# Hybrid decoder step: the gates and the levels of gated attention between the slots of the mixing projection, and a ring of cached pages that grows from 16 to 20, 24 and 28

## The chip, the cores and the metric

The kernel runs on one core of one Trainium2 chip. The metric is the device time of one execution in microseconds (us). The core has five engines that run side by side, each with its own queue of instructions that it takes in order, and they wait for one another by counting semaphores: TensorE (PE, matrix products and transposes), VectorE (DVE), ScalarE (ACT), GpSimd (POOL) and SyncE (SP, which here only issues transfers). The trace tells PE's weight loads (PEld) apart from its products. TensorE's clock has two levels, 1.2 and 2.4 GHz, and the profile gives the granted clock as a share of the higher one.

## What is computed

One inference step of one layer, for a prompt of 256 tokens and eight samples of 8 new tokens each (320 columns in all), with a model width of 1024:

```
x <- LN(alpha*x + 1/2*(1+g1)*SwiGLU_1(x*(1+s1)+b1))
x <- LN(alpha*x + (1+g2)*W_o[MoBA heads | GLA heads](x*(1+s2)+b2))
x <- LN(alpha*x + 1/2*(1+g3)*SwiGLU_2(x*(1+s3)+b3))
```

The middle sub-layer is the one that matters here. A projection w_mix_in (1024 x 3088) gives, for each token, queries, keys and values of 8 MoBA heads, queries, keys (4 heads of 64) and values (4 of 128) of gated linear attention (GLA), a GLA output gate, and 16 columns from which the forget gates come:

```
qm, km, vm, qg, kg, vg, gg, rg = split(h @ w_mix_in)
qm, km = rope_partial(qm, pos), rope_partial(km, pos)
log_a = log_sigmoid(rg @ w_gk_up + b_gk) / 16
```

MoBA, for a sample: mean of the keys of each block of 256 of the 2048 cached tokens, the three best blocks for each query and head, softmax over these and the new tokens. The cache is paged: 16 pages of 128 tokens for each sample, found through a page table, for K and for V. GLA: within a chunk, weights q_i k_j exp(b_i - b_j) for j <= i, where b is the running sum of log_a, plus a state that each sample brings and takes along. The results are y of prompt and samples, the new K and V rows and the GLA states, all float32.

## The kernel before

All products of weights are made in three parts (high x high, high x low, low x high) with weights and inputs split in a high part, rounded by ACT, and a low part, the remainder, which DVE subtracts. Weights come in "slots" of 1 MB, of which four fit in `raw`. The order of slots is the table at line 73 (A1, F1, O1, A2, MI, MO, F2, O2): conditioning, first feed-forward, its output, more conditioning, then MI, the mixing projection (12 slots, two output tiles of 128 rows each), MO, the output projection of the mixer (4 slots), and the second feed-forward. `high(t)` (ACT) and `low(t)` (DVE, line 1485) split slot t; there are two buffers each of `wh` and `wl`, so that slot n+2 is split when slot n is used. `pair_slot` multiplies a slot on PE: for each of two tiles 16 products with the high part of the weights and 8 with the low one. It puts the tiles in two of the banks B0 to B3; ACT copies them from there to `M`.

During MI, ACT does two copies to `M` and one `high` in each slot, DVE one `low` and, in the first eight slots, two instructions of `stream`, which rebuild the residual X. After the 12 slots stand, in the order of the program:

- the gates: 24 products for the 16 columns ("rg", lines 1026 to 1028), two groups for "z" (line 1034), on ACT an Exp and a Ln, on DVE a minimum, a subtraction and two running sums, which give `bb`
- rope of the eight q and k tiles (line 1040 on PE, 1952 to 1954 on DVE), and "nat": nine groups of transposes that turn V of GLA, V and K of MoBA back to token rows (lines 1047, 1054)
- the attention of the samples, in four pairs i of samples, into which all the rest is woven in 20 numbered steps, `mix(0)` to `mix(19)`

For one pair PE does, for j = 0 to 3: `turn_keys` twice (4 pages each, one for each sample of the pair, 16 transposes, line 823, copied to `kT` by ACT or DVE as `on_act` says), then `scores(i, j)` (line 834). DVE reduces the scores (`block_values`), then `choose(i)` picks the blocks, ACT makes the exponentials (`exps`), PE turns the probabilities (`turn_probs`, line 854) and multiplies them with the V pages (`values(i, 0)`, `values(i, 1)`, 16 pages each, line 872), and `pick_heads` with `out_high` and `out_low` writes the result to Hh and Hl. The order interleaves pairs: `values(i, 0)`, keys (i+1, 2), `values(i, 1)`, scores (i+1, 2), keys (i+1, 3), scores (i+1, 3), keys (i+2, 0) and so on.

The steps of `mix(k)`: 0 to 6 are causal attention of the prompt (scores, softmax, turned probabilities, values). 7 to 12 are the six "levels" of GLA: at level lv PE multiplies scaled keys with scaled queries (`level`, line 927, two groups "ga" of banks), DVE applies a mask and adds (`level_masks`, lines 1835 and 1847), multiplies the next level's factors (`level_qk`, 1819, 1822) and forms the one after (`level_diff`, 1807, 1812, 1813), and ACT takes two exponentials (`level_exps`). 13 to 19 are GLA's output and state.

Two tables set what waits for what. `FILLS` is the list of all fills of the five banks B3 to B7 that this stage shares in turn: a fill waits until the bank's fill five before was read. `PAGE_GROUPS` is the order in which SP loads the pages, 64 groups of 4 pages (1 MB, four transfers of 256 KB). The pages land in `ring`, 16 pages or 4 groups; group n waits until group n-4 was used, and SP takes the groups strictly in order (`load_pages`, line 548). The ring lies where `raw` lay, so the first groups wait for the last slots of MI. `M`, 24 x 320 elements a partition, and `W`, 9088 elements, hold the mixer's data.

The line that holds the ring's rule:

```
                    if kind == "k":
                        sp.wait_ge(tp_filled, FILL_AT[("k", i, g, bi, 3)] + 1)
                    else:
                        sp.wait_ge(v_used, v_index(i, bi, g) + 1)
```

## Time and profile before

| | us |
|---|---|
| median of 3 runs | 1030.9 (1025.99 to 1033.26) |
| profiled execution | 1030.04 |
| its span, first to last instruction | 1027.9 |
| PE busy in the span | 934.5 (91%) |
| PEld, DVE, ACT, POOL busy | 810.5, 547.0, 357.3, 28.0 |
| mean granted clock | 0.941 |

The profiled execution is one of its own; 2.1 us of its time lie outside the span. Positions below are us from the span's start. The mixing projection runs from 337 to 424, the samples' attention with all that is woven into it to 717. PE busy is a sum of modelled intervals, so a stretch in which PE is fully busy can still run at half its clock.

### The profile page before, as it was taken

The page shows a single profiled execution, that of the slowest core. Times are in us where ns is not written, and L with a number is a line of the kernel's source. Part 1 is how long each engine was busy: PE and PEld are TensorE (multiplying, and loading weights), DVE is VectorE, ACT ScalarE, POOL GpSimd, SP SyncE. Part 2 cuts the span into 40 slices and gives each one's busy share as a digit, 9 for nine tenths or more (in the row PEclk, how much of TensorE's full clock was granted, in tenths as well). Part 3 has the DMA queues.
Part 4 walks back from the last instruction along what each step waited for, and adds up shares of the span by engine and source line. Part 5 has one row for each costly group of instructions (what it writes and reads, how often), then busy time and mean ns, then how long its engine had stood idle before and what let it go on. Part 6 is the DMA issues. An engine that isn't in the chain of part 4 may idle for free. (4 is left out here: it accounts for less than half of the span.)

```text
span 1027.9 us, 17283 instructions
## 1 busy us (share of the span) xinstructions
PE 934.5 (91%) x6991; PEld 810.5 (79%) x6991; DVE 547.0 (53%) x841; ACT 357.3 (35%) x506; POOL 28.0 (3%) x34
## 2 busy tenths in 40 slices
PE   6999999999999999978786679685989999999997
PEld 2588888888996899845565567554959999999994
DVE  0435444444654744487557644273575666555664
ACT  1423232323343433437424232340243323323333
POOL 0000000000100000010000000000300000000000
PEclk9899999999999999989887898886999999999999
DMA  9799888885557651747595692889433655533521
GB/s 330 233 304 260 247 237 249 236 228 149 144 169 254 195 163 63 248 151 246 167 375 179 208 365 103 298 282 325 127 82 83 164 145 143 152 106 115 147 58 51
DMA packets 214886, 199.93 MB, mean 195 GB/s; under 512 B 9570, under 2 KB 161262, under 8 KB 214679
## 3 DMA queue, kind: packets, MB, share of 16 engines
q1 hardware_dynamic: 213412, 194.99, 61.7%
q0 software_dynamic: 704, 2.49, 0.7%
q10 hardware_dynamic: 690, 1.35, 0.4%
q8 instruction: 55, 0.90, 0.4%
q14 instruction: 25, 0.20, 0.1%
HBM read 195.00 MB, written 3.80 MB: 193 GB/s over the span
## 5 line engine op out<-in xcount | busy, mean ns | idle before, releaser
L622 PE MATMUL B<-Hh,wh 128*128 128x320 f32 x912 | 272.7, 313 | 0.6 <-issue 0.6
L1491 DVE TENSOR_TENSOR wl<-raw,wh 128x2048 fp32r<-128x2048 f32 x90 | 207.3, 2305 | 120.6 <-ACT wh L1146 113.8
L623 PE MATMUL B<-Hl,wh 128*128 128x320 f32 x912 | 270.6, 310 | 0.0
L1146 ACT ACTIVATE wh<-raw 128x2048 fp32r<-128x2048 f32 x90 | 172.2, 1913 | 148.3 <-PE B L627 115.9
L622 PEld LDWEIGHTS B<-Hh,wh 128*128 128x128 f32 x912 | 172.4, 189 | 10.0 <-issue 10.0
L623 PEld LDWEIGHTS B<-Hl,wh 128*128 128x128 f32 x912 | 172.4, 189 | 0.0
L627 PE MATMUL B<-Hh,wl 128*128 128x320 f32 x912 | 152.5, 309 | 0.0
L627 PEld LDWEIGHTS B<-Hh,wl 128*128 128x128 f32 x912 | 138.9, 188 | 0.0
L622 PE MATMUL B<-Gh,wh 128*128 128x320 f32 x352 | 106.0, 315 | 2.5 <-DVE Gl L1617 2.5
L623 PE MATMUL B<-Gl,wh 128*128 128x320 f32 x352 | 105.5, 313 | 0.0
L823 PE MATMUL B<-cst,ring 128*128 128x128 f32 x512 | 73.3, 307 | 29.9 <-DMA ring<-in_cache_k 11.8
L823 PEld LDWEIGHTS B<-cst,ring 128*128 128x128 f32 x512 | 66.7, 160 | 40.7 <-issue 15.1
L1146 ACT ACTIVATE sg<-B 128x320 f32<-128x320 f32 x46 | 20.1, 438 | 211.1 <-PE B L627 195.7
L1609 DVE TENSOR_TENSOR hf<-sg,B 128x320 f32<-128x320 f32 x44 | 21.4, 487 | 124.7 <-ACT sg L1146 124.7
L622 PEld LDWEIGHTS B<-Gh,wh 128*128 128x128 f32 x352 | 67.7, 192 | 2.7 <-DVE Gl L1617 2.7
L623 PEld LDWEIGHTS B<-Gl,wh 128*128 128x128 f32 x352 | 67.6, 192 | 0.0
L872 PE MATMUL B<-ring,PT 128*32 128x128 f32 x1024 | 39.2, 313 | 21.5 <-DMA ring<-in_cache_v 21.5
L1696 DVE COPY kT<-B 128x512 f32<-128x512 f32 x64 | 40.8, 682 | 32.2 <-PE B L823 32.2
L627 PE MATMUL B<-Gh,wl 128*128 128x320 f32 x352 | 56.8, 309 | 0.0
L872 PEld LDWEIGHTS B<-ring,PT 128*32 128x32 f32 x1024 | 31.8, 125 | 28.0 <-DMA ring<-in_cache_v 25.4
L627 PEld LDWEIGHTS B<-Gh,wl 128*128 128x128 f32 x352 | 52.9, 187 | 0.0
L1146 ACT ACTIVATE kT<-B 128x512 f32<-128x512 f32 x64 | 34.8, 608 | 39.9 <-PE B L823 39.8
(235 smaller groups left out, 931.0 us busy)
## 6 DMA issues: line engine op xcount, KB each, us to landing
raw<-in_w_ffn_in SPq DMA_DIRECT2D x88, 512.0 KB, 6.1
raw<-in_w_ada SPq DMA_DIRECT2D x72, 512.0 KB, 4.9
ring<-in_cache_k SPq DMA_DIRECT2D x128, 256.0 KB, 4.2
ring<-in_cache_v SPq DMA_DIRECT2D x128, 256.0 KB, 4.5
raw<-in_w_ffn_out SPq DMA_DIRECT2D x32, 384.0 KB, 3.4
raw<-in_w_mix_in SPq DMA_DIRECT2D x24, 512.0 KB, 4.8
raw<-in_w_ffn_out SPq DMA_DIRECT2D x32, 320.0 KB, 4.1
raw<-in_w_mix_out SPq DMA_DIRECT2D x4, 512.0 KB, 7.7
```

The lines of the kernel that those rows point to most:

```text
L622: pe.matmul(out, w, xh[k], start=start and k == 0, stop=False)
L623: pe.matmul(out, w, xl[k], start=False, stop=False)
L627: m = pe.matmul(out, w, xh[k], start=False, stop=stop and k == last)
L823: m = pe.transpose(bank[:, c * P:(c + 1) * P], ring[:, at + p, c * P:(c + 1) * P], ident)
L872: m = pe.matmul(out[32 * c:32 * c + 32, :], PT[:, 4 * g + p, 32 * c:32 * c + 32], ring[:, at + p, c * P:(c + 1) * P], start=(g == 0 and p ...
L1146: return act.activation(out, in_, func, **kw)
L1491: dve.tensor_tensor(wl[:, wbuf(n), :], raw_view(n), f32(wh[:, wbuf(n), :]), ALU.subtract).then_inc(lo_ready, 1)
L1609: step(dve.tensor_tensor(hf[:, j, :], sg[:, j, :], B[2 * j][:, 0:N], ALU.mult))
L1696: dve.tensor_copy(kT[:, bi, :, p * P:(p + 1) * P], tb(key).rearrange("p (c s) -> p c s", c=HP)).then_inc(tp_dve, 1)
```

## The change

It moves work and adds buffers. Both are tables and order of code.

- The gates, rope, the turned-back K, V and GLA's V, and the six levels now stand in the "gaps" between the 12 slots of MI: `gap(n)` on PE, and loops over n on ACT and DVE, unrolled. `MI_TILES` loads the tiles of GLA's q and k as slots MI+4 and MI+5 and MoBA's V as slots MI+6 and MI+7. The residual's `stream` runs for all eight tiles after slot 0. The fills of this part use banks B4 to B7 only, as the projection has B0 to B3.
- In the samples' attention, `AT_POINT` sets the remaining steps: points of the order at which `mix(6 .. 11)` stood are closed up, so that mix(2) to mix(6) come one or two points later and mix(13) to mix(19) earlier by up to three.
- `state_gla` is loaded after the levels, as `masked` now lies in its place. pp and ppT lie in Z.
- The pages get three more places of 4 pages: `IN_H`, the halves of Hh and Hl that GLA's output fills at the end (free from the end of MI until pair 2's values), `IN_M` in `M` (from group 28, the first V of pair 1, on) and `IN_W` in `W` (from group 44, the first V of pair 2, on). `place_groups` gives each group the place that was given longest ago. SP's order of the groups is as it was. The second slot of MO is loaded two groups later than before.
- `on_act` shares the copies to `kT` in another way, `exps` is cut in two so that ACT copies keys between, and DVE does `out_low` and the first keys of the next pair ahead of `choose`.

```
+MI_TILES = [0, 1, 2, 3, 6, 7, 4, 5, 8, 9, 10, 11]
...
+GAPS[0] = [("rg",)]
+GAPS[1] = [("z", 0), ("z", 1), ("rot", 0), ("rot", 1)]
...
+GAPS[5] = [("nk", t) for t in range(3)]
+GAPS[8] = [("nv", t) for t in range(3)]
+GAPS[10] = [("nvg", t) for t in range(3)]
+for _lv in range(6):
+    GAPS[6 + _lv] += mix_fills(7 + _lv)
...
+AT_POINT = {0: 0, 1: 1, 3: 2, 4: 3, 5: 4, 6: 5, 8: 6, 9: 12, 10: 13, 11: 14, 13: 15, 14: 16, 15: 17, 16: 18, 18: 19}
...
+IN_RING, IN_H, IN_M, IN_W = range(GROUPS), GROUPS, GROUPS + 1, GROUPS + 2
+BEGIN_AT = {GROUP_AT[("v", 1, 0, 0)]: IN_M, GROUP_AT[("v", 2, 0, 0)]: IN_W}
+LAST_IN = {IN_H: GROUP_AT[("v", 2, 3, 0)], IN_M: GROUP_AT[("k", 3, 3, 1)], IN_W: GROUP_AT[("v", 3, 0, 0)]}
+    for n in range(len(PAGE_GROUPS)):
+        if n in BEGIN_AT:
+            queue.insert(0, BEGIN_AT[n])
+        queue = [b for b in queue if n <= LAST_IN.get(b, n)]
+        b = queue.pop(0)
+        queue.append(b)
...
+BANK = [4 + n % 4 if n < IN_MI else 3 + (n - IN_MI) % 5 for n in range(len(FILLS))]
...
-        return p % 2 == 0 if j >= 2 else j == 0
+        if j == 0:
+            return i == 0 or p != 3
+        return p % 2 == 0 if j >= 2 else (bi == 1 and p % 2 == 1)
...
+                if GROUP_BEFORE[n] is not None:
+                    wait_used(GROUP_BEFORE[n])
+                elif b == IN_H:
+                    sp.wait_ge(used, MI + 12)
+                elif b == IN_M:
+                    sp.wait_ge(tp_filled, FILL_AT[("po", 3)] + 1)
...
-                if n == len(PAGE_GROUPS) - 4:
-                    for k in range(2):
-                        load_wide(At(MO + k), mix_out, 256 * k)
+                if n in (len(PAGE_GROUPS) - 4, len(PAGE_GROUPS) - 2):
+                    k = 0 if n == len(PAGE_GROUPS) - 4 else 1
+                    load_wide(At(MO + k), mix_out, 256 * k)
...
+            for n in range(12):
+                act.wait_ge(used, MI + n + 1)
+                if n < 10:
+                    act_(M[:, c, :], B[b0][:, 0:N]).then_inc(act_step, 1)
+                    act_(M[:, c + 1, :], B[b0 + 1][:, 0:N]).then_inc(out_read, 1)
+                    high(At(MI + n + 2))
...
+                if 6 <= n <= 9:
+                    level_exps(n - 4)
...
+            for n in range(12):
+                if n == 1:
+                    gates_in()
+                if 1 <= n <= 4:
+                    rope(2 * n - 2)
+                    rope(2 * n - 1)
+                if n >= 6 and n < 11:
+                    level_masks(n - 6)
+                if n < 10:
+                    low(At(MI + n + 2))
...
+                if 6 <= n <= 10:
+                    level_qk(n - 5)
+                    if n <= 9:
+                        level_diff(n - 4)
...
                 block_values(i, 3)
-                choose(i)
                 if i >= 1:
                     out_low(i - 1)
                 if i + 1 < NPAIR:
                     keys_dve(i + 1, 0, 0)
                     keys_dve(i + 1, 0, 1)
-                    mix(m0)
+                choose(i)
```

How the instructions stand. On PE, before, this follows the 24 products of the 16 columns and the first keys, all after the twelfth slot (z, then rotations of q and k, and transposes of V):

```order
L1034 MATMUL B<-hf,wgk 128x320 x2
L1040 MATMUL B<-M,cst 128x320 x2
L823 MATMUL B<-cst,ring 128x128 x16
L1040 MATMUL B<-M,cst 128x320
L1047 MATMUL B<-cst,M 128x128 x4
L1040 MATMUL B<-M,cst 128x320
L1047 MATMUL B<-cst,M 128x128 x4
L1040 MATMUL B<-M,cst 128x320
L1047 MATMUL B<-cst,M 64x128 x4
```

In the changed kernel the transposes of GLA's V and level 4 stand between slots MI+10 and MI+11 of the projection (line 691, 692 and 696 are the products with the slots' weights, 991 the level):

```order
L691 MATMUL B<-Hh,wh 128x320
L692 MATMUL B<-Hl,wh 128x320
L696 MATMUL B<-Hh,wl 128x320 x8
L1114 MATMUL B<-cst,M 128x128 x8
L1114 MATMUL B<-cst,M 64x128 x4
L991 MATMUL B<-Z 128x128 x8
L691 MATMUL B<-Hh,wh 128x320
L692 MATMUL B<-Hl,wh 128x320
```

So twelve transposes and eight products of a level now come between the last low product of a slot and the first high one of the next; the other gaps are built alike.

On DVE, before, the last slots of the projection hold a `low` (line 1491) and at most two instructions of `stream`, then the gate's product and the gates:

```order
L1491 TENSOR_TENSOR wl<-raw,wh 128x2048
L1569 SCALAR_TENSOR_TENSOR X<-Z,prmT,rstd 128x320
L1571 TENSOR_SCALAR X<-X,prmT 128x320
L1491 TENSOR_TENSOR wl<-raw,wh 128x2048 x2
L1675 TENSOR_TENSOR M<-M,B 128x320 x4
L1944 TENSOR_SCALAR Z<-B,prmT 128x320 x2
```

In the changed kernel, between the `low` of slots MI+8 and MI+9 (line 1595), stand a level's factors, differences, masks and sum:

```order
L1595 TENSOR_TENSOR wl<-raw,wh 128x2048
L1908 SCALAR_TENSOR_TENSOR Z<-M,Z 128x2x256
L1911 TENSOR_TENSOR Z<-M,Z 128x2x256
L1896 TENSOR_TENSOR Z<-W 128x2x256
L1901 TENSOR_SCALAR Z<-Z 128x2x256
L1902 TENSOR_SCALAR Z<-Z 128x2x256
L1924 TENSOR_TENSOR W<-B,cst 128x4x128 x2
L1936 TENSOR_TENSOR W<-W 128x1024
L1595 TENSOR_TENSOR wl<-raw,wh 128x2048
```

Seven instructions for a level have come between two subtractions of weights, each of which the products of a slot wait for.

On DVE in the attention of pair 1, before, the end of `choose` (lines 1729 to 1734) stands ahead of `out_low` of pair 0 (1766) and of a level:

```order
L1729 TENSOR_TENSOR small<-small 128x8
L1730 TENSOR_REDUCE small<-small 128x1
L1733 TENSOR_SCALAR small<-small 128x1
L1734 TENSOR_SCALAR small<-small 128x8
L1766 TENSOR_TENSOR Hl<-B,Hh 128x4x16
L1835 TENSOR_TENSOR M<-B,cst 128x4x128 x2
L1847 TENSOR_TENSOR W<-W,M 128x1024
L1819 SCALAR_TENSOR_TENSOR Z<-M,Z 128x2x256
```

In the changed kernel `out_low` (1855) and two key copies (1785) come right behind the reductions of the scores (1792, 1794), and `choose` begins after them (1812):

```order
L1792 TENSOR_REDUCE small<-B 128x2
L1794 TENSOR_REDUCE small<-B 128x2
L1855 TENSOR_TENSOR Hl<-B,Hh 128x4x16
L1785 COPY kT<-B 128x4x128 x2
L1812 TENSOR_TENSOR small<-small 128x64
L1813 TENSOR_TENSOR small<-small 128x64
```

The reading of the bank that `pick_heads` filled has moved ahead of ten small instructions, and the level behind it is gone.

## Rows read from the trace of the kernel before

**Rows 1.** Stretches: length, busy of PE, PEld, DVE, ACT, POOL, clock, DMA share, GB/s
```profile
337.00:424.10 87.10, 86.19 (x581) 84.83 (x579) 40.48 (x47) 32.24 (x42) 0.00 (x0) 1.00 0.47 149
424.10:451.70 27.60, 22.61 (x128) 13.82 (x125) 17.48 (x33) 16.05 (x30) 2.69 (x4) 0.89 0.55 180
451.70:504.20 52.50, 43.09 (x369) 31.27 (x365) 42.94 (x113) 29.24 (x86) 0.00 (x0) 0.96 0.62 201
504.20:574.20 70.00, 51.18 (x588) 39.94 (x586) 38.75 (x75) 22.89 (x54) 0.52 (x1) 0.79 0.69 241
574.20:644.00 69.80, 59.94 (x645) 47.76 (x643) 35.71 (x70) 20.05 (x50) 0.00 (x0) 0.87 0.69 242
644.00:693.20 49.20, 35.77 (x438) 27.89 (x437) 24.05 (x65) 20.05 (x41) 0.72 (x1) 0.83 0.88 303
693.20:717.00 23.80, 13.19 (x277) 10.53 (x276) 6.17 (x11) 3.00 (x3) 1.18 (x1) 0.68 0.94 320
```

**Rows 2.** Waits of PE, 427.3 to 717: total us, times, longest
```profile
PE B L872 <- DMA ring<-in_cache_v: 21.5, 12, 5.7
PE B L823 <- DMA ring<-in_cache_k: 11.8, 3, 4.5
PE B L823 <- DVE kT L1696: 7.2, 2, 3.8
PE B L823 <- DVE Hl L1766: 6.3, 2, 4.5
```

**Rows 3.** Two stretches of 5 us, columns as in rows 1
```profile
525.00:530.00 5.00, 4.22 (x68) 2.89 (x64) 0.00 (x0) 0.00 (x0) 0.00 (x0) 0.50 1.05 387
...
640.00:645.00 5.00, 5.00 (x57) 3.81 (x59) 3.33 (x10) 1.93 (x5) 0.00 (x0) 1.00 0.00 0
```

**Rows 4.** Groups by line, PE, 424.1 to 448.1: busy us, mean ns, idle before
```profile
L1040 PE MATMUL B<-M,cst 128*128 128x320 f32 x16 | 6.2, 478 | 2.0 <-DVE M L1954 2.0
...
L1047 PE MATMUL B<-cst,M 128*128 128x128 f32 (+1 forms) x24 | 3.6, 273 | 0.0
...
L1054 PE MATMUL B<-cst,M 128*128 128x128 f32 (+1 forms) x12 | 2.2, 350 | 1.9 <-DVE M L1954 1.9
L1034 PE MATMUL B<-hf,wgk 16*128 16x320 f32 x4 | 1.3, 454 | 0.0
```

**Rows 5.** Timeline of PE at three places: start, length, instruction, idle before
```profile
448.14 3.64 PE L834 MATMUL B<-kT,Qz 128*32 128x512 f32 x16 [1.12 <-ACT knew L1146]
...
535.80 1.16 PE L927 MATMUL B<-Z 64*128 64x128 f32 x16
...
549.60 2.00 PE L927 MATMUL B<-Z 64*128 64x128 f32 x16
```

**Rows 6.** Groups by line, PE, whole span: the levels
```profile
L927 PE MATMUL B<-Z 64*128 64x128 f32 x88 | 9.2, 367 | 3.8 <-DVE PT L1752 3.8
```

**Rows 7.** Groups by line, DVE, whole span
```profile
L1491 DVE TENSOR_TENSOR wl<-raw,wh 128x2048 fp32r<-128x2048 f32 x90 | 207.3, 2305 | 120.6 <-ACT wh L1146 113.8 <-PE B L627 6.7
...
L1835 DVE TENSOR_TENSOR M<-B,cst 128x512 f32<-128x512 f32 x8 | 5.5, 692 | 8.8 <-PE B L927 8.6
...
L1847 DVE TENSOR_TENSOR W<-W,M 128x1024 f32<-128x1024 f32 x4 | 4.9, 1224 | 0.1
...
L1807 DVE TENSOR_TENSOR Z<-W 128x512 f32<-128x512 f32 (+1 forms) x6 | 4.3, 713 | 0.2
L1819 DVE SCALAR_TENSOR_TENSOR Z<-M,Z 128x512 f32<-128x512 f32 (+1 forms) x6 | 4.3, 712 | 0.3
...
L1813 DVE TENSOR_SCALAR Z<-Z 128x512 f32<-128x512 f32 x5 | 2.1, 427 | 0.2
```

**Rows 8.** Groups by line and shape, ACT, whole span
```profile
L1146 ACT ACTIVATE wh<-raw 128x2048 fp32r<-128x2048 f32 x90 | 172.2, 1913 | 148.3 <-PE B L627 115.9 <-DMA raw<-in_w_ffn_in 32.4
...
L1146 ACT ACTIVATE M<-B 128x320 f32<-128x320 f32 x24 | 9.2, 435 | 53.7 <-PE B L627 49.7 <-PE B L648 4.0
...
L1146 ACT ACTIVATE Z<-Z 128x512 f32<-128x512 f32 x10 | 5.7, 620 | 2.5 <-DVE Z L1813 2.5
```

More of the change, by code:

```diff
@@ L480, in _, with wait_used @@
             mix_out = a["w_mix_out"].rearrange("(k p) f -> p k f", p=P)
+            def wait_used(n):
+                kind, i, g, bi = PAGE_GROUPS[n]
+                if kind == "k":
+                    sp.wait_ge(tp_filled, FILL_AT[("k", i, g, bi, 3)] + 1)
+                else:
+                    sp.wait_ge(v_used, v_index(i, bi, g) + 1)
             def wait_free(t):
@@ L872, in values @@
                             m = pe.matmul(out[32 * c:32 * c + 32, :], PT[:, 4 * g + p, 32 * c:32 * c + 32],
-                                          ring[:, at + p, c * P:(c + 1) * P], start=(g == 0 and p == 0), stop=False)
+                                          at[p][:, c * P:(c + 1) * P], start=(g == 0 and p == 0), stop=False)
                     m.then_inc(v_used, 1)
@@ L1046, in _, with turn_back @@
+            def turn_back(name, base):
+                for t, (t0, tn) in enumerate(TILES):
+                    bank = turn_bank((name, t))
                     for x in range(4):
@@ L1048, in _, with gap, point @@
                     m.then_inc(tp_filled, 1)
-                    n += 1
-            pe.wait_ge(roped, 8)
-            for t0, tn in TILES:
-                bank = turn_bank(("nat", n))
-                for x in range(4):
-                    m = pe.transpose(bank[0:tn, x * P:(x + 1) * P], M[:, CK + x, t0:t0 + tn], ident)
-                m.then_inc(tp_filled, 1)
-                n += 1
+            def gap(n):
+                if n == 0:
+                    gates()
+                if n == 1:
+                    gates_up()
+                if 1 <= n <= 4:
+                    rotate(2 * n - 2)
+                    rotate(2 * n - 1)
+                if n == 5:
+                    pe.wait_ge(roped, 8)
+                    turn_back("nk", CK)
+                if n == 8:
+                    pe.wait_ge(out_read, READ["MI"] + 8)
+                    turn_back("nv", CV)
+                if n == 10:
+                    pe.wait_ge(out_read, READ["MI"] + 10)
+                    turn_back("nvg", CVG)
+                if n >= 6:
+                    level(n - 6)
+            first_slot(At(MI), "wide", 0, 1)
+            gap(0)
+            for n in range(1, 12):
+                pe.wait_ge(out_read, READ["MI"] + n - 1)
+                pair_slot(At(MI + n), "wide", 2 * (n % 2))
+                gap(n)
+            pe.wait_ge(out_read, READ["MI"] + 12)
+            turn_keys(0, 0, 0)
+            turn_keys(0, 0, 1)
+            def point(x):
+                if x in AT_POINT:
+                    mix(AT_POINT[x])
             pe.wait_ge(new_ready, 2)
@@ L1063, in _ @@
             turn_keys(0, 1, 1)
-            mix(0)
+            point(0)
             scores(0, 1)
@@ L1263, in keys_act @@
                             act.wait_ge(s_out, 4 * i + j)
+                        else:
+                            act.wait_ge(used, MI + 12)
                         act_(kT[:, bi, :, p * P:(p + 1) * P], tb(key).rearrange("p (c s) -> p c s", c=HP)
@@ L1963, in _, with point @@
+            def point(x):
+                if x in AT_POINT:
+                    mix(AT_POINT[x])
             block_values(0, 0)
```

426 lines of the change are left out of this document (218 added, 208 removed).

## The prediction

> **What bounds the kernel now.** I read the page first: PE is busy for 91% of the span, but its line in the 40 slices falls from 9 to between 5 and 8 in the part from 424 to 717. So I cut that part into stretches at each pair's first product with V pages [rows 1]. From 337 to 424, the projection, PE is full at clock 1.00, while DVE works 40.5 and ACT 32.2 of 87.1 us and the transfers take 0.47. From 424.1 to 717.0 PE is idle for 67.1 us (5.0, 9.4, 18.8, 9.9, 13.4 and 10.6 by stretch), and the clock is below 1. Idle time costs twice: after it PE works for a while at 1.2 GHz. Sixteen level products take 1.16 us at one place and 2.00 at another, where PE had just stood idle [rows 5]. A mean clock c means that a share 2(1-c) of a stretch ran at the lower level; if busy time is spread evenly, half of that share of the busy time is the loss: 1.7, 10.7, 7.8, 6.1 and 4.2 us in the five stretches from 451.7.
>
> The waits of PE come next [rows 2]. Of the 67 us, 33.3 end with a transfer of pages (21.5 for V, 11.8 for K), and most of the others with a bank that DVE or ACT has yet to read. Yet the transfers aren't at their limit throughout: stretches of 5 us with 387 GB/s stand beside others with 0 [rows 3]. SP waits for room in the ring in the second kind, and PE for pages in the first. The ring of 4 MB is thus too short for the bursts of the order, in which 10 groups (10 MB) are used by two `values` and one pair of `turn_keys`.
>
> **Part 1: work moved into the projection.** Moved from behind it are z, rope and the transposes: 1.3 + 6.2 + 3.6 + 2.2 = 13.3 us of PE [rows 4]. The 24 products for the gates took 3.3 us behind the projection (24 times 0.14, the pace of all products of 320 columns there) and take as long in gap 0. The levels are 9.2 us of PE in 88 products [rows 6], at 1.16 us for 16 some 6.4, with the samples' small ones 6.9. PE is full in the projection, so all is added there: 87.1 us grow by 23.5 and the twelfth slot and its level end at 424.1 + 23.5 = 447.6. Of the 22.6 us that PE was busy from 424.1 to 451.7, what is not 3.3, 3.6 of scores or the moved parts is the first keys. Then come, in a row, the sigmoid and the product with it on ACT and DVE (some 1.2 us that the 24 products hid), the first keys, now all copied by ACT, 3.8 + 0.3, and the first scores, 1.9. That ends at 454.8; before, it was 451.7, with scores of 3.64 us at the lower clock [rows 5]. I take +3 us; between 0, if the gaps overlap, and +8, if each of 11 gaps stalls by half a microsecond.
>
> DVE pays per slot with a level: masks 2 x 0.69 + 1.22, `low` 2.31, factors 2 x 0.71, differences 0.71 + 2 x 0.43, together 7.9 us [rows 7], against a slot with its level of some 7.0 (87.1 / 12 is 7.3, and the first slot is the longer one) + 1.2 = 8.2. ACT pays 2 x 0.44 + 1.91 + 2 x 0.62 = 4.0 [rows 8]. Both fit, DVE barely. But there is a ring of waits: the exponentials wait for the differences, the next copies to M and `high` wait behind the exponentials, `low` for `high`, factors and differences come behind `low`. Its period is 1.24 + 0.87 + 1.91 + 2.31 + 1.42 + 1.57 = 9.3 us, so DVE and ACT fall behind by about 1.1 us in each of five slots. A `low` is ready some 7 us before its slot's products want it, so 5.5 us of delay cost nothing; if that cover is gone, each further microsecond is one of PE.
>
> In the attention the levels' 6.9 us of PE vanish, and on DVE six sets of about 5 us (29 in all), on ACT 7.5. That is work behind which copies of keys and reductions of scores waited.
>
> **Part 2: the order of what stays.** The steps of the prompt come later and those of GLA's output earlier. This moves PE's time between stretches and adds none. `out_low` ahead of `choose` frees the bank for which keys waited 6.3 us in two waits [rows 2]; on the last pair it puts about 1.2 us before the exponentials, but a DVE product of 1.5 us that stood there has gone to an earlier point. I count zero for the pair.
>
> **Part 3: more room for pages.** At 387 GB/s a group takes 2.71 us. For pair 0's burst the ring has five groups, for pair 1's six, for pair 2's six with a seventh coming, and the early ones are loaded while PE is at keys. I laid group by group against PE's order at the higher clock: from pair 0's first `values` to pair 1's, PE wants 51.2 busy - 10.7 of clock loss - 4.6 for the four sets of levels that lie there + 7 for steps that the table moves in = 43 us, and 16 groups want 43.4, so the two run side by side with some 3 to 5 us of waits; to pair 2's, PE wants 59.9 - 7.8 - 1.6 - 1 = 49.5 and nothing waits for pages; to pair 3's, the second `values` still waits some 3.5 us, and the choice of blocks 5. In the tail nothing is gained: 4 MB were left to load before, now three groups and the second slot of MO, and the last group is released at the same point. 23.8 us [rows 1] become 24.5.
>
> A rule of the Trainium skill speaks against part 3. Rows 3 show 387 GB/s over 5 us with pages of 256 KB. "DMA: Bandwidth & Descriptors", section Specifications, puts a core's share of the memory at about 358 GB/s. By the rule a group takes 2.93 us and 44 groups 10 us more than by the row. The trace doesn't agree with it here, and I go by the row.
>
> **The sum.** From 451.7 to 693.2 PE is busy 190.0 us [rows 1]. Without 26.3 of clock loss and 6.9 of levels 156.8 are left. Before, idle time of 51.5 came on top. Now I put idle time at 6 + 5 + 4 + 9 = 24 and clock loss at 9: 189.8 in place of 241.5, so -51.7. With +3 at the start and +0.7 in the tail: -48. The profiled execution took 1030.0, so 982; the median of the runs shown is 0.9 above that, within its own spread of 7 us. The bounds: if DVE and ACT keep all 27 us of the waits that are theirs and pages half of theirs, idle is 39 and clock loss 18, 214 us, and with +8 and +1 the sum is 1012. Below, idle of 10 and clock loss of 4 give 171, just above what 44 groups allow (46 + 1 + 119 = 166): 963.
>
> **Rivals.**
> - Handoffs bound the attention. For it: 34 of the 67 us are not waits for transfers, and the banks and their order are as before. Against it: a third of DVE's work there has gone (29 of 141 us [rows 1]). Then idle is 34 and clock loss 15: 206 us, so 1030 - 36 + 4 = 998 to 1005.
> - Pages come too late all the same. SP takes the groups in order, so one group without room stops all behind it; for it speaks that the extra places join only at groups 4, 28 and 44, and that the first burst has just one more. If the bursts wait as before and only part 1 counts: 6.9 of levels, 7 of waits for banks, about 5 of clock, less 3: 1012 to 1016.
> - Transfers and PE overlap nearly without waits: 960 to 967.
> - Slower. The ring of waits in the projection costs more than its cushion. If each of its six handoffs adds half a microsecond, the period is 12.3 against 8.2; after two slots the 7 us are used up, PE idles 4 us in each of three slots, falls to 1.2 GHz, and the last five slots and their levels take up to twice 8.2: 12 + 41. The first pages, which need these slots' places, are late by as much. 982 + 53 is 1035. It decides when the period passes some 10 us.
>
> **How the numbers follow.** The forecast, 968 to 995, has 0.6. The handoffs (995 to 1008) have 0.2, late pages 0.07, the good case below 968 0.07, slower 0.04, and 0.02 is for anything else. Range 966 to 1008, which leaves out about 0.2. One per cent (10 us) is about what a measurement can tell. Faster by more than that (below 1020) takes all but the last two: 0.92; within 0.04; slower 0.04.
>
> **What would show it.** The twelfth slot should end near 447 and the first scores near 455, with no idle over 1 us between slots. PE's idle time from there to MO should be about 35 us, waits for pages below 18 (9 of them in the tail), and no wait for line 1855's bank above 1 us. The stretches between the first `values` of pairs 0 to 3 should be near 50, 56 and 37. MO should begin near 669. I am wrong if PE stands idle between slots, if a stretch from pair to pair stays above 60, or if the transfers stay at 0.7.

## The result and the profile after

The changed kernel takes 997.9 us in the median of 4 runs (993.2 to 1002.5), the kernel before 1030.5 beside it: ratio 0.969, 95% interval 0.963 to 0.975. That is 32 us faster, inside the range of 966 to 1008, but 16 us above the forecast of 982. Measured again beside other kernels (run 11), it had 997.2 in 6 runs, ratio 0.964 (0.961 to 0.968). One execution of all that follow, of the kernel after_ring16, took 2001.2 us at a clock of 1.00, for a reason that no trace shows, and is left out of that kernel's time. The profiled execution took 995.8 us, its span 993.8; PE is busy for 916.5 us of it (934.5 before), at a mean clock of 0.965 (0.941 before).

The stretches of the kernel after answer to those of [rows 1], cut at the same places: end of slot 12's products, end of the first scores, first V product of pairs 0 to 3, start of MO.

```profile
334.00:454.20 120.20, 111.81 (x749) 104.08 (x747) 86.84 (x126) 51.42 (x74) 2.70 (x4) 0.96 0.40 129
454.20:462.70 8.50, 6.21 (x57) 4.45 (x56) 0.98 (x2) 5.34 (x13) 0.00 (x0) 1.00 0.73 245
462.70:512.90 50.20, 41.61 (x355) 29.22 (x353) 40.20 (x106) 28.16 (x82) 0.00 (x0) 0.97 0.75 253
512.90:567.00 54.10, 44.87 (x584) 34.89 (x585) 23.87 (x54) 19.60 (x49) 0.00 (x0) 0.93 0.88 312
567.00:619.40 52.40, 50.20 (x592) 40.06 (x595) 27.77 (x65) 25.15 (x54) 0.72 (x1) 0.93 0.97 345
619.40:660.60 41.20, 32.07 (x424) 24.26 (x423) 22.78 (x57) 11.94 (x33) 1.17 (x1) 0.83 0.89 312
660.60:683.80 23.20, 11.64 (x277) 9.51 (x277) 3.54 (x8) 4.51 (x4) 0.00 (x0) 0.72 1.01 330
```

The reader is to see three things. The four stretches between the first scores and pair 3 have shrunk from 241.5 to 197.9 us, and their share of transfers has gone from 0.6 to 0.9 up to 0.75 to 0.97. The projection, which was full, now has 8.4 us in which PE stands, and a clock of 0.96. And the tail is as long as it was. PE's waits from 424 to 690 answer to [rows 2]:

```profile
PE B L936 <- DMA ring<-in_cache_v: 16.0, 6, 6.5
...
PE B L975 <- DVE PT L1841: 3.6, 1, 3.6
PE B L991 <- ACT W L1240: 3.2, 1, 3.2
...
PE B L887 <- DMA ring<-in_cache_k: 1.8, 1, 1.8
...
PE B L936 <- DMA M<-in_cache_v: 1.5, 1, 1.5
...
PE B L936 <- DMA pages_l<-in_cache_v: 0.8, 1, 0.8
```

Pages are waited for 20.1 us (with 1.5 for a page in M and 0.8 for one in Hl, which the profile calls pages_l) where it was 33.3. The waits of 7.2 and 6.3 us for VectorE have become 1.8 and 0.3. New are the wait of line 991, and its twin at 421, ahead of that window. The timeline of PE in the projection shows both at the level products (line 991):

```profile
421.49 2.08 PE L991 MATMUL B<-Z 64*128 64x128 f32 x16 [3.60 <-ACT W L1240]
431.36 1.16 PE L991 MATMUL B<-Z 64*128 64x128 f32 x16
444.29 1.16 PE L991 MATMUL B<-Z 64*128 64x128 f32 x16 [3.23 <-ACT W L1240]
```

and the timeline of ACT shows what it did before it read the bank in question (the copy to W):

```profile
417.26 1.15 ACT L1240 ACTIVATE Z<-Z 128x512 f32<-128x512 f32 x2 [5.42 <-DVE Z L1902]
418.32 0.74 ACT L1240 ACTIVATE M<-B 128x320 f32<-128x320 f32 x2
418.95 1.91 ACT L1240 ACTIVATE wh<-raw 128x2048 fp32r<-128x2048 f32 x1
420.75 1.08 ACT L1240 ACTIVATE W<-B 128x512 f32<-128x512 f32 x2
```

In gaps 8 and 10 PE makes three turned-back tiles and then two level fills: five fills for four banks. The fifth needs the first one's bank. In gap 8 ACT reads that only behind the exponentials, the copies to M and `high`. In gap 10 there is no `high` any more; there the exponentials and the two sigmoids stand ahead of the read, and between them a load of ACT's function table:

```profile
441.60 1.28 ACT L1240 ACT_TABLE_LOAD   x1
```

Behind both waits PE works for a while at the lower clock (last section).

**How far two profiles can be compared.** The eleven kernels with the moved work are alike up to the projection, yet its first product stands anywhere between 332.0 and 336.0 in their twelve traces. So below I compare lengths between two events of one trace. The first slot comes in two forms, too: in half of the traces PE waits in it six times for some 0.26 us for ACT's Hh, in the others three times. The first form makes the projection 2.4 us longer. The changed kernel's first profile is of the longer form, its second and that of level_first are of the shorter. "The attention" is from the end of the first scores to the end of the last values: 218.6 us in the changed kernel, 221.0 in its second profile; differences of 2 us mean nothing there.

### The profile page after: what moved, and what is told of

Read it like the earlier page. It is cut to its first block, busy times and chain, and to the rows that moved or that the text cites. A ratio compares the mean times of both kernels' runs of the same rounds, so it can differ in the third digit from the quotient of the medians.

```text
span 993.8 us, 17303 instructions
## 1 busy us (share of the span) xinstructions
PE 916.5 (92%) x6991; PEld 797.4 (80%) x6991; DVE 545.8 (55%) x839; ACT 359.2 (36%) x509; POOL 28.0 (3%) x34
## 4 chain that ended last, share of the span: by engine, by line
PE 80%; DVE 9%; ACT 4%; DMA 3%; issue 3%; SPq 2%; ACTq 0%; DVEq 0%
PE B L691 19%; PE B L692 18%; PE B L696 18%; PE B L751 4%; PE B L887 3%; PE B L898 2%; PE B L936 2%; PE B L760 2%; PE B L791 2%; SPq L619 2%; DMA ring<-in_cache_v 1%; PE B L775 1%; PE B L1017 1%; ACT kT L1240 1%; PE B L717 1%
## 5 line engine op out<-in xcount | busy, mean ns | idle before, releaser
L691 PE MATMUL B<-Hh,wh 128*128 128x320 f32 x912 | 275.7, 316 | 0.6 <-issue 0.6
L691 PEld LDWEIGHTS B<-Hh,wh 128*128 128x128 f32 x912 | 173.7, 190 | 11.0 <-issue 10.2
L1240 ACT ACTIVATE sg<-B 128x320 f32<-128x320 f32 x46 | 20.1, 437 | 207.3 <-PE B L696 193.8
L887 PE MATMUL B<-cst,ring 128*128 128x128 f32 x432 | 52.8, 276 | 7.1 <-DMA ring<-in_cache_k 1.8
L887 PEld LDWEIGHTS B<-cst,ring 128*128 128x128 f32 x432 | 46.8, 141 | 14.5 <-issue 6.4
L936 PE MATMUL B<-ring,PT 128*32 128x128 f32 x672 | 26.0, 306 | 18.0 <-DMA ring<-in_cache_v 16.0
L751 PE MATMUL B<-raw,cpk 128*32 128x512 f32 x288 | 39.2, 622 | 0.3 <-ACT cpk L1240 0.3
```

The costliest lines, as they stand in the source:

```text
L691: pe.matmul(out, w, xh[k], start=start and k == 0, stop=False)
L751: m = pe.matmul(B[4 + pair % 2][32 * k:32 * k + 32, :], cpk[:, 4 * half + k, :], v[:, k, :], start=(half == 0), stop=(half == 1))
L887: m = pe.transpose(bank[:, c * P:(c + 1) * P], at[p][:, c * P:(c + 1) * P], ident)
L936: m = pe.matmul(out[32 * c:32 * c + 32, :], PT[:, 4 * g + p, 32 * c:32 * c + 32], at[p][:, c * P:(c + 1) * P], start=(g == 0 and p == 0), ...
L1240: return act.activation(out, in_, func, **kw)
```

## The experiments

The theory after the first look had four parts. The projection lost 8 us by the order of fills in gaps 8 and 10. The first stretch lost 3.6 us by one handoff (line 975). What is left of waits for pages is set by the transfers. And both parts of the change count, which I could not tell apart from one profile.

**1. Levels ahead of the turned-back tiles (level_first).**

```
-_lv: GAPS[6 + _lv] += mix_fills(7 + _lv)
+_lv: GAPS[6 + _lv] = mix_fills(7 + _lv) + GAPS[6 + _lv]
 def gap(n):
+    if n >= 6: level(n - 6)
     if n == 8: ... turn_back("nv", CV)
     if n == 10: ... turn_back("nvg", CVG)
-    if n >= 6: level(n - 6)
```

> The changed kernel with one order turned round: in gaps 8 and 10 of the projection TensorE makes the level's two fills first and the three turned-back tiles behind them. Theory A (two late reads: three turned-back fills and two level fills are five fills for four banks, and ScalarE, which must read the first of them, comes late because it waits for VectorE's level differences): the two stalls of 3.6 and 3.2 us at L991 go, the clock behind them stays high, the first scores end at 455 to 457 instead of 462.7, and the time is 988 to 992 us against 998 of the changed kernel. Rival B (the ring of waits between VectorE, ScalarE and TensorE sets the pace, the banks do not): the same idle time comes back at the level's first wait for VectorE or at the next slot's weights, first scores at 461 to 463, time within 2 us of the changed kernel's.

Measured: 987.4 us, ratio 0.956 (0.949 to 0.962). The timeline of PE has no wait left at the levels:

```profile
414.88 1.16 PE L991 MATMUL B<-Z 64*128 64x128 f32 x16
424.46 1.16 PE L991 MATMUL B<-Z 64*128 64x128 f32 x16
432.79 1.16 PE L991 MATMUL B<-Z 64*128 64x128 f32 x16
```

From its start the projection with the first scores takes 115.4 us, against 128.0 in the changed kernel and 125.6 in its second profile, whose first slot has the same form. From the first level on it is 53.2 us against 63.3 in both profiles. So the order is worth 10.2 us: 6.8 are the two waits, the other 3.4 were PE at the lower clock behind them (the last section has the rows). The forecast for the whole length was 117.7; the three further kernels with the levels first and no additions (lf_mo1, probs_first, combo) have 117.8 with the longer form of the first slot. Without the two waits, part 1 comes out as I had worked out, or up to 2 us better. Theory A holds; the time lies just under its window, and the first scores end at 451.0.

These are still five fills for four banks. But now the fifth, a turned-back tile, needs the bank of the level's first fill, which VectorE reads at once (its masks). It is not the count alone that costs, but who has to read the first one, and what stands before that read.

**2. The exponentials one slot later (exps_late).**

```
 for n in range(12):
+    if n == 10: level_exps(5)
     ... copies to M, high ...
+    if 7 <= n <= 9: level_exps(n - 5)
     ...
-    if 6 <= n <= 9: level_exps(n - 4)
```

> The changed kernel with the exps of levels 2 to 5 one slot later on ScalarE, behind the slot's copies and its high half, so that ScalarE no longer waits there for VectorE's differences. Theory A (late reads): ScalarE comes to the turned-back tiles in time although there are still five fills for four banks; the stalls at L991 fall under 1 us each, first scores end at 455 to 458, time 988 to 993. Rival B (the exps one slot later make VectorE's factors late instead, so the ring is as long as it was): TensorE now waits at the level's first instruction for VectorE, 3 us or more in gaps 8 to 11, first scores at 461 or later, time 997 or more. Rival C (bank count alone): both stalls at L991 stay over 3 us.

Measured: 996.6 us, ratio 0.964 (0.958 to 0.970), as the changed kernel. Nearest is rival C, though by its letter ("over 3 us") it misses in one gap: PE still waits in gap 8, for 2.96 us, and in gap 10, for 3.24:

```profile
417.04 1.16 PE L991 MATMUL B<-Z 64*128 64x128 f32 x16 [2.96 <-ACT W L1240]
...
439.85 2.08 PE L991 MATMUL B<-Z 64*128 64x128 f32 x16 [3.24 <-ACT W L1240]
```

and yet ACT doesn't wait for VectorE ahead of gap 8 any more, only for PE's slot:

```profile
412.81 0.77 ACT L1240 ACTIVATE M<-B 128x320 f32<-128x320 f32 x2 [4.72 <-PE B L696]
413.46 1.91 ACT L1240 ACTIVATE wh<-raw 128x2048 fp32r<-128x2048 f32 x1
415.26 1.15 ACT L1240 ACTIVATE Z<-Z 128x512 f32<-128x512 f32 x2
416.30 1.08 ACT L1240 ACTIVATE W<-B 128x512 f32<-128x512 f32 x2
```

So my picture of the two waits was half wrong. ACT is late by its own work in the slot (0.65 + 1.8 + 1.04 us, and half a microsecond for the first tile), and the lateness behind VectorE's differences added 0.6 us. What costs is that the fifth fill asks for the bank within that time. In gap 10 the exps, which wait for VectorE, and the table load still come first, so that wait is no test.

**3 to 5. The parts and the places apart.** after_ring16 takes part 3 back:

```
-BEGIN_AT = {GROUP_AT[("v", 1, 0, 0)]: IN_M, GROUP_AT[("v", 2, 0, 0)]: IN_W}
-queue = list(IN_RING) + [IN_H]
+BEGIN_AT = {}
+queue = list(IN_RING)
```

> The changed kernel with the ring of 16 pages of the kernel before (no places in Hh and Hl, M and W; both weight tiles MO and MO+1 in front of the last four groups). Theory A (the work that left the page stretches would have gone straight into waits for pages): the waits for pages that the extra places took away return, 25 to 45 us in all, the time is 1012 to 1028 us. Rival B (shorter page stretches alone are worth most of the gain, the extra places little): time 998 to 1006, waits for pages under 25 us.

Measured: 1008.3 us in the median of three executions (1009.7 with the one of 2001.2), ratio 0.976 (0.967 to 0.984). Waits for pages are back to 29.2 us:

```profile
PE B L937 <- DMA ring<-in_cache_v: 16.3, 10, 4.7
PE B L888 <- DMA ring<-in_cache_k: 12.9, 8, 3.2
```

before_ring puts part 3 alone into the kernel before (page_at, place_groups and the waits that go with them). The place in W joins at `("v", 2, 0, 1)`, group 50, the first values of pair 2's second sample. That is six groups later than in the change (group 44), and not one, as the expectation has it, so this kernel has somewhat less of part 3:

> The kernel before with the extra places of the change alone (Hh and Hl from the start, M from the values of pair 1 on, W one group later than in the change, since the gated outputs are made later there). Gates and levels stay between the stretches of pages. Theory A (pages hide behind the work that is still there once they can be loaded ahead): most of the waits of 24 us for pages in the stretches go and the clock rises, time 1000 to 1012 us. Rival B (the places alone just move the waits, because slots are given back no sooner): time 1020 to 1030. If both parts were simply additive, this gain and that of the kernel with 16 places sum to the 32 us of the whole.

Measured: 1023.3 us, ratio 0.991 (0.987 to 0.994): rival B by the time. Pages are still waited for 29.8 us, 24.9 in the ring, 3.1 in Hl and 1.8 in M, against 33.3 before, and the waits for VectorE stand where they were:

```profile
PE B L918 <- DMA ring<-in_cache_v: 20.3, 9, 6.4
PE B L869 <- DVE kT L1743: 7.2, 2, 3.9
PE B L869 <- DVE Hl L1813: 6.3, 2, 4.5
PE B L869 <- DMA ring<-in_cache_k: 4.6, 2, 2.5
```

after_ring20 has the place in Hh and Hl (`queue = list(IN_RING) + [IN_H]`) but none in M and W:

> The changed kernel with 20 places only (the ring and the place in Hh and Hl; none in M and W; both weight tiles MO and MO+1 ahead of the last four groups). The kernel with 16 places took 1009.7 us, the changed one with 28 took 998 (of another call). Theory A (each place gives time in which transfers run on while TensorE is at something else, so the first one, there from the start, is worth the most): 1002 to 1005 us, waits for pages 22 to 26 us. Rival B (the places in M and W, which join for the bursts of pairs 1 and 2, carry the gain): 1007 to 1010, waits as with 16 places (29 us).

Measured: 1001.4 us, ratio 0.969 (0.965 to 0.974), with 21.3 us of waits for pages: nearer to theory A, whose windows both miss by about a microsecond. From 16 to 20 places it is some 7 us, from 20 to 28 between 0 and 5; the intervals of the ratios overlap in both steps, so only the falling waits (29.2, 21.3, 20.1 us) are clear. The two ratios 0.976 and 0.991 multiply to 0.966; the whole change has 0.964 to 0.969. So the parts are about independent: some 25 us are the moved work (16 to 34 by its interval), some 10 the places. For the moved work neither of my two expectations fitted: the time lies between the two windows, and the waits of 29 us are those of theory A.

**6. Half the transfers (half_pages).**

```
+PAGES_IN = [4 if n < 12 or GROUP_BEFORE[n] is None else 2 for n in range(len(BUF))]
-for j in range(4): sp.dma_start(page_at(b, j), ...)
+for j in range(PAGES_IN[n]): sp.dma_start(page_at(b, j), ...)
```

> The changed kernel with half the transfers: from group 12 on, a group that is not the first in its place loads two of its four pages, and the other two keep what stood there; the work of every engine is unchanged. Theory A (after the change, transfers at their full rate bound the stretches from pair 1 on, and what is left of idle time in them are waits for pages): the waits for pages fall from 18 to under 4 us, the clock there goes up, the time is 972 to 982 us. Rival B (handoffs between TensorE, VectorE and ScalarE hold the stretches at the same length and the pages come under them anyway): 992 to 997 us, with the idle time moved to banks and scores. If the second stretch (54.1 us) hardly moves and the third and fourth do, both hold, each in its place.

Half of the pages of these groups are left out, and the products run on what stood in their places. Measured: 977.6 us, ratio 0.946 (0.941 to 0.950); 4.6 us of waits for V pages are left, in the tail. The stretches between the ends of the first values of pairs 0, 1, 2 and 3, first of this kernel, then of the changed kernel in its second profile:

```profile
518.00:564.90 46.90, 44.86 (x584) 36.70 (x581) 23.69 (x51) 19.35 (x48) 0.00 (x0) 0.93 0.62 207
564.90:618.90 54.00, 51.79 (x588) 41.62 (x588) 30.95 (x72) 23.80 (x51) 0.72 (x1) 0.91 0.53 169
618.90:651.30 32.40, 28.24 (x430) 22.60 (x427) 21.59 (x51) 14.24 (x33) 1.17 (x1) 0.89 0.69 229
```

```profile
515.30:572.50 57.20, 47.69 (x580) 37.53 (x580) 23.69 (x51) 19.35 (x48) 0.00 (x0) 0.88 0.90 317
572.50:626.60 54.10, 51.89 (x592) 41.73 (x589) 30.95 (x72) 23.80 (x51) 0.72 (x1) 0.91 0.89 313
626.60:666.10 39.50, 31.05 (x426) 23.14 (x427) 21.08 (x51) 14.24 (x33) 1.17 (x1) 0.83 0.97 336
```

Each theory has its place, but not where I had put them: the first and third row shrink by 10 and 7 us, the middle one not at all. There PE is busy for 51.9 of 54.1 us, whatever the transfers do. A transfer share of 0.9 beside a nearly full PE is no bound; the same share beside an idle PE is one. (The first profile of the changed kernel had 53.8 us in the first row. All ten other traces with the moved work and full transfers have 56 to 60; why that one was short there is not known.)

**7. Part 2 taken back (part2_undone).**

```
 block_values(i, 3)
+choose(i)
 if i >= 1: out_low(i - 1)
 ... keys_dve(i + 1, 0, 0), keys_dve(i + 1, 0, 1)
-choose(i)
...
-exps(i, 0, 6) ... exps(i, 6, 9)
+exps(i, 0, 9)
```

The shares of the key copies and block_values(i + 1, 0) go back as well; the new places of the prompt's and GLA's steps stay.

> The changed kernel with part 2 taken back: on VectorE the choice of blocks ahead of the last outputs' low half and of the next pair's first keys, block_values(i+1, 0) ahead of the keys behind it, on ScalarE all nine exps of a pair in one piece, and the old shares of the key copies. Theory A (the prediction's zero: the order pays nothing by itself, since the waits that it shortens are followed by others that end as late): within 4 us of the changed kernel, 994 to 1002. Rival B (it is the order that removed the two waits of 7.2 and 6.3 us for VectorE that stood in the kernel before): these waits come back at the first keys of pairs 2 and 3, 9 us or more in all, and the time is 1004 to 1010.

Measured: 1000.3 us, ratio 0.967 (0.962 to 0.972): no difference that these runs can tell. The wait for `out_low`'s bank comes back, but with 3.6 us instead of 6.3:

```profile
PE B L885 <- DVE Hl L1852: 3.6, 2, 1.8
```

The wait for key copies at the same line is 1.3 us (1.8 in the changed kernel, 7.2 before). So the rest did not go with this order, but with what this kernel keeps: the levels moved off VectorE and the new places of the steps. No run tells these two apart.

**8. MO+1 behind the last pages (lf_mo1),** on level_first:

```
-if n in (len(PAGE_GROUPS) - 4, len(PAGE_GROUPS) - 2): load MO, MO + 1
+if n == len(PAGE_GROUPS) - 4: load MO
 ...
-for k in range(2, 4): load_wide(At(MO + k), ...)
+for k in range(1, 4): load_wide(At(MO + k), ...)
 ACT: high(MO), out_high, high(MO + 1)
```

> The kernel level_first with one more order turned round: the load of the weight tile MO+1 (1 MB) goes behind the last page group instead of between the third and second from the end, and ScalarE makes its high half behind the last outputs. Theory A (in the tail transfers run at their full rate and 1 MB ahead of the last two groups delays both): the last values start 2 to 3 us earlier, MO starts 2 to 3 us earlier, MO+1's high half still comes in time: 984 to 986 us, against 987.4 of level_first. Rival B (MO+1 then lands too late for the second slot, which waits for it): the second slot of MO starts with a wait of 1 to 3 us and the time is 987 to 990.

Measured: 985.5 us, ratio 0.952 (0.947 to 0.956). The waits in the tail, first of level_first, then of this kernel:

```profile
662.66 1.94 PE L936 MATMUL B<-ring,PT 128*32 128x128 f32 x32 [5.06 <-DMA ring<-in_cache_v]
668.35 1.93 PE L936 MATMUL B<-ring,PT 128*32 128x128 f32 x32 [3.75 <-DMA ring<-in_cache_v]
```

```profile
661.97 1.79 PE L935 MATMUL B<-ring,PT 128*32 128x128 f32 x32 [0.49 <-DMA ring<-in_cache_v]
666.07 1.20 PE L935 MATMUL B<-ring,PT 128*32 128x128 f32 x32 [2.31 <-DMA ring<-in_cache_v]
```

From the end of the values of (3, 0) to that of (3, 1) it is 13.8 us instead of 17.8 (16.9 and 15.9 in the changed kernel's two profiles), and MO's second slot doesn't wait. All waits for pages from 655 on fall from 9.6 to 4.4 us. The median moves by 2 us, no more than its noise; the mechanism is shown by the trace, the gain of the whole is not.

**9. The ring of waits made longer (ring_longer),** on level_first:

```
 if 6 <= n <= 10: level_masks, low(n + 2)
+    for _ in range(3):
+        step(dve.tensor_tensor(hf[:, 1, :], X[:, 0, :], X[:, 1, :], ALU.add))
     level_qk(n - 5) ...
```

> The kernel level_first with three products of 320 columns more on VectorE, each waited for, in each of the five slots of the projection that have a level's factors (about 0.5 us each, so 1.5 us a slot and 7.5 in all); their result is used by nobody. Theory A (the prediction's ring of waits: VectorE and ScalarE fall behind by what their period exceeds TensorE's slot, and after some 7 us of delay each further microsecond is TensorE's): TensorE waits 4 to 7 us in gaps 8 to 11, the clock falls behind it, first scores end 5 to 9 us later than 451.0, time 992 to 996. Rival B (the delay has more room, since VectorE and ScalarE still stand idle in each slot: VectorE waited 1.2 and 0.5 us for TensorE's levels, ScalarE 3.4 to 5.4 us for VectorE): under 2 us of wait on TensorE, time within 3 us of level_first's 987.4.

Measured: 991.6 us, ratio 0.961 (0.956 to 0.966), which by its interval could be that of level_first. The trace is clearer: the projection with the first scores is 123.1 us long, against 117.8 in the three kernels with the levels first and the same form of the first slot. PE waits in gaps 8, 9 and 10, for the level's factors:

```profile
PE B L991 <- DVE Z L1911: 4.7, 3, 2.1
```

`low` on VectorE shows the period:

```profile
421.38 2.29 DVE L1595 TENSOR_TENSOR wl<-raw,wh 128x2048 fp32r<-128x2048 f32 x1 [1.14 <-ACT wh L1240]
431.83 2.29 DVE L1595 TENSOR_TENSOR wl<-raw,wh 128x2048 fp32r<-128x2048 f32 x1 [1.15 <-ACT wh L1240]
```

10.45 us, of which the additions take 1.57: 8.88 without them, where I had added up 9.3. The ring of waits is real. But it costs nothing in level_first for another reason than I gave. I had set its period against a slot of 8.2 us; PE's slots with their levels alternate between 8.33 and 9.58 us (level_first above), since gaps 8 and 10 hold turned-back tiles too, and their mean of 8.96 is about as long as the ring. Nor is there a cushion of 7 us. That is how early `low` is for its slot's products; what PE comes to wait for are the factors of a level, and in level_first these are ready 0.9, 1.6 and 0.9 us before PE's level in gaps 8, 9 and 10. Of the 6.3 us that were added up to gap 10, PE waited 4.7, so 1.6 were free. The slower rival's mechanism is thus shown at a period of 10.45, and it starts after less than 2 us of delay. The clock, though, stayed at 1.00 behind these waits.

**10. Copies of the probabilities first (probs_first),** on level_first, for pair 0:

```
-point(4); block_values(1, 1); probs_dve(0, 0); probs_dve(0, 1)
+mix(3, norms=False); probs_dve(0, 0); probs_dve(0, 1)
+prompt_norm(4); prompt_norm(5); block_values(1, 1)
```

> The kernel level_first with one order turned round on VectorE for pair 0: the two norms of the prompt's softmax and the reductions of scores(1, 1) go behind the copies of the turned probabilities, not ahead of them. Theory A (the wait of 3.6 us for PT goes, but in this stretch the pages are late too, so the time comes back as waits for transfers): L975's wait falls to about 1 us, the waits for pages at the first values and the keys behind them grow from 6.9 us by as much, the values of (0, 1) end within 1 us of 523.5, and the time is that of level_first within 3 us. Rival B (a wait gone is a wait gone): the values of (0, 1) end 2 to 3 us earlier relative to the first scores, time 984 to 985.

Measured: 982.1 us, ratio 0.950 (0.946 to 0.955). The wait at line 975 and the largest of the page waits behind it, in level_first and here:

```profile
497.99 0.43 PE L975 MATMUL B<-Z,W 128*64 128x128 f32 x2 [3.60 <-DVE PT L1841]
...
521.14 1.94 PE L936 MATMUL B<-ring,PT 128*32 128x128 f32 x32 [2.46 <-DMA ring<-in_cache_v]
```

```profile
494.31 0.43 PE L975 MATMUL B<-Z,W 128*64 128x128 f32 x2 [1.09 <-DVE PT L1841]
...
517.23 1.62 PE L936 MATMUL B<-ring,PT 128*32 128x128 f32 x32 [2.51 <-DMA ring<-in_cache_v]
```

Theory A is refuted. The page waits behind it sum to 7.4 us, against 6.9, so they hardly grew, and the values of (0, 1) end 69.4 us behind the first scores, not 72.5. So these waits are not those for a stream that runs at its own pace all along. SP, in turn, waits for PE's V products to give back places. In level_first it stood 12.3 us for them, until 502.6, and the transfers ran dry:

```profile
495.00:500.00 5.00, 2.01 (x17) 1.84 (x18) 4.33 (x14) 2.09 (x9) 0.00 (x0) 0.91 0.01 3
```

The pages in Hl for which PE waits next were asked for here, in level_first and in this kernel:

```profile
509.47 0.85 SPq L619 DMA_DIRECT2D pages_l<-in_cache_v  x2
```

```profile
504.93 0.85 SPq L619 DMA_DIRECT2D pages_l<-in_cache_v  x2
```

That is 58.5 and 55.1 us behind the first scores: 3.4 us earlier. When PE comes earlier, such a page is asked for earlier and lands earlier; once asked for, the burst runs at full rate (388 GB/s from 515 to 525 in level_first), so the waits inside it stay as they are. Before the run I had taken these waits for the other kind. How much of the 5 us in the median is this edit is open, for the intervals of the two ratios overlap: in the trace it is 3.1.

**11 and 12. The changed kernel again, and the sum of what helped (combo).**

> The changed kernel itself once more, so that it has times on the same chip and in the same rounds as the versions built on it. It measured 0.969 of the kernel before; expected 0.964 to 0.974. If its stretch from the first values of pair 0's end to those of pair 1, 53.8 us in its first profile, comes out at 57 to 60 as in the kernels with 16 and 20 places and in both kernels with the level first, then that first profile was a lucky one there.

Measured: 997.2 us, ratio 0.964 (0.961 to 0.968); the stretch named was 57.2 us, so the first profile was the exception there. The combo has the edits of 1, 8 and 10, and

```
-BEGIN_AT = {GROUP_AT[("v", 1, 0, 0)]: IN_M, ...}
+BEGIN_AT = {GROUP_AT[("v", 1, 2, 0)]: IN_M, ...}
```

> The version meant to beat both kernels: levels ahead of the turned-back tiles (level_first), MO+1's load behind the last group (lf_mo1), the copies of probabilities first (probs_first), and the place in M joins two groups later, at the third group of pair 1's values instead of the first, when TensorE has just left it, so that the queue does not stand for 7 us on that one place. Theory A (the queue's wait there costs pages later on): the wait for L977 on SP's queue falls from 7 us to under 2, page waits from pair 1's values to pair 2's shrink by 2 to 4 us, the time is 979 to 984. Rival B (VectorE and the handoffs hold those stretches, no page is waited for there): the SP wait goes and nothing else changes, 984 to 987, as lf_mo1 with 985.5.

Measured: 978.3 us, ratio 0.946 (0.942 to 0.950), against 0.964 for the changed kernel beside it: it beats both, the changed one by 19 us. The wait of SP's queue for line 977 has gone from 7.2 us in level_first to 0.8 (line 976 here), but the stretches behind it are as they were: 56.4 and 52.4 us from values to values, against 57.1 and 52.4 in level_first. For the place in M rival B's mechanism holds, though the time lies just under theory A's window: the gains of 8 and 10 on top of level_first, taken from their ratios, already come to 0.946.

## Why the prediction was right, and where it was off

**What bounds, and the sign.** Right. Idle time in the attention, half waits for pages and half handoffs, and the clock behind them, were the reserve, and both parts of the change draw on it.

**The content of the work.** Right. From 462.7 to 660.6 PE was busy for 168.75 us. Taking from each stretch its busy time times (1 - clock), 13.3 us in all, leaves 155.4; the prediction had 156.8. The projection without its waits took 115.4 to 117.8 us with the first scores, where the forecast had 117.7.

**"First scores at 454.8."** Here the largest step failed. They ended at 462.7. The prediction did not lay the fills of each gap against the four banks. "Each of 11 gaps stalls by half a microsecond" was the wrong shape for the upper bound: two gaps stall by more than three, and the clock pays again. Run 1 gives that back with 10 us.

**The ring of waits "covered by 7 us".** Right in its result, by luck in its numbers. The prediction had DVE and ACT fall behind by 1.1 us a slot, and 7 us in hand. Run 9 shows a ring of 8.9 us against slots of 8.96 in the mean, so nothing falls behind, and only 1.6 us in hand. With slots of 8.2 and a ring of 9.3, as it was summed, five slots would have brought 5.5 us of delay, more than that room, and PE would have waited.

**The stretches.** Forecast 46 to 47 (what the sum leaves), 50, 56, 37 and a tail of 24.5; measured 50.2, 54.1, 52.4, 41.2 and 23.2. The term "idle 24, clock loss 9" was mis-sized: it was 29.1 and 13.3. The first stretch misses by the wait of 3.6 us at line 975. I had counted it nowhere, though the changed table puts the prompt's softmax ahead of the copies of probabilities. The second and fourth miss by waits for pages (run 6), the third was taken too long. With +7.9 for the first scores, +8.1 for these four stretches and -1.3 for the tail, 982 becomes 996.7; the profiled execution had 995.8.

**The shares of the parts.** Here the prediction was wrong in both, with opposite signs. The rival in which only part 1 counts gave 1012 to 1016, so part 3 was to bring 30 or more. Parts 1 and 2 alone brought about 25 us and part 3 some 10. I had moved the waits for pages wholesale to part 3. What fits is the reading of run 10: less work ahead of a product that frees a place brings the pages sooner too. For the whole of part 1 that is argued, not shown.

**Part 2 at zero.** Within the noise (run 7).

**Signs named beforehand.** Idle time from the first scores to MO was 40.7 us against 35; waits for pages 20.1 against "below 18", 8.4 of them in the tail; the wait for the bank of line 1855 is 0.3, as said. MO began at 683.8 instead of 669. "No idle over 1 us between slots" failed, and was the sign that showed where to look.

**Rivals.** By its time the result is that of the handoffs (998 to 1005), in the part of the range that had a chance of 0.2, not in the 968 to 995 that had 0.6. But what kept it there was neither banks in the attention nor VectorE alone: half of the miss lay in the projection. The slower one needs a period that the kernel does not reach (8.9 us; at 10.45 it shows).

## What to carry to other kernels

Where work is moved into a place that was full, count per step not only each engine's time but also the buffers: how many fills stand before the first one is read, which engine reads it, and what that engine does ahead of it. Here an order of two lines was worth 10 us, as much as 12 more pages of memory. And of a wait for a transfer ask first whether the transfer is slow or was asked for late. If it was asked for late, because the same engine gave the place back late, then a microsecond saved in front of it need not be eaten up by that wait: 2.5 us less of one wait brought 3.1 here (run 10).

## What was not expected

Transfers that run on are as fast in the attention with 28 places as in the single window of [rows 3]. The four windows of 5 us from 525 to 545 of the changed kernel have 382 to 387 GB/s, the three from 600 to 615 have 387 to 392, columns as above:

```profile
600.00:605.00 5.00, 4.85 (x33) 4.04 (x36) 3.26 (x13) 2.76 (x7) 0.00 (x0) 1.00 1.05 392
```

By the Trainium skill's "DMA: Bandwidth & Descriptors", Specifications, a core's share is about 358 GB/s; the trace is 7 to 10% above it here too, with one core at work. The Trainium skill's section "Bandwidth" on the same page says that about 358 is what each of two cores gets when both stream, so that it is no limit for the one here, and has 425 GB/s for a single core with transfers of 16 MB; no run here shows two cores at work, or such sizes.

Both waits at the levels cost the clock, but the first products behind a wait do not always show it. In the changed kernel 16 level products took 2.08 us behind 3.60 us of idle time, and 1.16 behind 3.23. The fall came all the same, with the next products, and lasted about as long:

```profile
421.40:425.00 3.60, 3.51 (x22) 3.31 (x23) 1.38 (x2) 1.37 (x3) 1.28 (x2) 0.53 0.18 71
445.40:448.80 3.40, 3.40 (x15) 3.40 (x14) 3.21 (x5) 0.00 (x0) 0.00 (x0) 0.50 0.86 318
```

In exps_late it is the other way round, late behind 2.96 us and at once behind 3.24. Behind the waits of 2.06, 0.55 and 2.06 us of ring_longer it did not fall. Why it comes at once or late stays open.
